# Stick-breaking attention in a hybrid trunk block: key blocks of 128 with a separate sum tile, against key blocks of 127 with the sum in row 0

## The reference, cut to what matters

```python
z = einsum('bqhd,bkhd->bhqk', q_blk, kh) * scale
mask = key_pos[None, :] < q_pos[:, None]
log_1m_beta = where(mask, log_sigmoid(-z), 0.0)
between = cumsum(log_1m_beta, axis=3, reverse=True) - log_1m_beta
weights = where(mask, exp(log_sigmoid(z) + between), 0.0)
out = einsum('bhqk,bkhd->bqhd', weights, vh)
```

## Time and profile before

| | us |
|---|---|
| median of 3 runs | 1556.61 (1551.15 to 1557.23) |
| profiled execution, time | 1550.32 |
| profiled execution, span from first to last instruction | 1548.5 |
| `heads`, first exp of a unit to the first product of `Ahead` | 522.8 to 730.6 |

### The profile page before, as it was taken

How to read it: one execution, slowest core, us unless ns; L and a number is a source line. 1 busy time by engine, 2 the same in 40 slices (tenths; PEclk the granted TensorE clock), 3 DMA queues, 4 the chain that set the end, 5 groups by cost and what they waited for, 6 DMA issues and landing times.

```text
span 1548.5 us, 27297 instructions
## 1 busy us (share of the span) xinstructions
PE 1466.1 (95%) x11281; PEld 1138.3 (74%) x11281; DVE 670.5 (43%) x1072; ACT 525.2 (34%) x947; POOL 308.9 (20%) x412
## 2 busy tenths in 40 slices
PE   7989989989898899999999999999999999999997
PEld 5767777767677555554777788888888888888876
DVE  6244151555653454655464424242332424242337
ACT  5423231433323476877443403021120403021132
POOL 6674615422332252523001000000000000000000
PEclk9999989999999999999999999999999999999999
DMA  6454413423224513021433302021120302111014
GB/s 201 138 149 120 127 42 97 125 59 86 70 68 109 166 25 78 6 76 62 163 109 109 109 0 95 14 68 41 38 70 0 98 10 75 34 57 51 27 60 171
DMA packets 134969, 124.10 MB, mean 80 GB/s; under 512 B 20829, under 2 KB 112154, under 8 KB 134874
## 3 DMA queue, kind: packets, MB, share of 16 engines
q1 hardware_dynamic: 88588, 92.90, 19.4%
q10 hardware_dynamic: 46286, 29.84, 6.8%
HBM read 97.88 MB, written 24.84 MB: 79 GB/s over the span
## 4 chain that ended last, share of the span: by engine, by line
PE 47%; DVE 2%; ACT 1%; DMA 1%; issue 1%; POOLq 0%; SPq 0%; DVEq 0%; ACTq 0%
PE all_ps_b L2018 22%; PE all_ps_b L1995 22%; PE all_ps_b L1585 2%; DMA bk_acc<-in_w_out 1%; POOLq L1605 0%; DVE bk_acc L1872 0%; PE all_ps_b L1988 0%; ACT bk_acc L1773 0%; DVE bk_acc L1882 0%; DVE bk_w1L L1843 0%; DVE bk_acc L1868 0%; DVE all_hL L1888 0%; DVE all_gL L1914 0%; ACT bk_rect L1804 0%; DVE bk_acc L1945 0%
## 5 line engine op out<-in xcount | busy, mean ns | idle before, releaser
L1924 DVE TENSOR_TENSOR bk_acc<-bk_acc,all_ps_b 128x512 f32<-128x512 f32 x128 | 87.9, 687 | 274.4 <-PE all_ps_b L2018 274.2
L1995 PE MATMUL all_ps_b<-all_hH,bk_w1L 128*128 128x512 f32 x512 | 200.2, 391 | 5.1 <-PE all_ps_b L2018 2.1
L2018 PE MATMUL all_ps_b<-bk_w2H,all_gL 128*128 128x512 f32 x512 | 199.4, 389 | 2.5 <-DVE all_gL L1914 2.5
L1995 PE MATMUL all_ps_b<-all_hH,bk_w1H 128*128 128x512 f32 x512 | 199.4, 389 | 0.0
L1995 PE MATMUL all_ps_b<-all_hL,bk_w1H 128*128 128x512 f32 x512 | 199.3, 389 | 0.0
L2018 PE MATMUL all_ps_b<-bk_w2L,all_gH 128*128 128x512 f32 x512 | 199.2, 389 | 0.0
L2018 PE MATMUL all_ps_b<-bk_w2H,all_gH 128*128 128x512 f32 x512 | 199.2, 389 | 0.0
L1207 PE MATMUL fr_ps_F<-fr_hH,fr_wL 128*128 128x512 f32 (+1 forms) x416 | 174.7, 420 | 6.5 <-POOL fr_wL L459 6.4
L459 POOL TENSOR_TENSOR fr_wL<-fr_raw,fr_wH 128x256 fp32r<-128x256 f32 (+1 forms) x208 | 161.9, 809 | 26.0 <-ACT fr_wH L504 22.7
L1207 PE MATMUL fr_ps_F<-fr_hL,fr_wH 128*128 128x512 f32 (+1 forms) x416 | 164.8, 396 | 0.0
L1207 PE MATMUL fr_ps_F<-fr_hH,fr_wH 128*128 128x512 f32 (+1 forms) x416 | 164.5, 395 | 0.0
(11 more groups left out here) (349 smaller groups left out, 2281.9 us busy)
## 6 DMA issues: line engine op xcount, KB each, us to landing
fr_raw<-in_w_in ACTq DMA_DIRECT2D x37, 512.0 KB, 4.2
bk_raw<-in_w_ff SPq DMA_DIRECT2D x32, 512.0 KB, 4.3
all_raw<-in_w_ff SPq DMA_DIRECT2D x32, 512.0 KB, 3.7
projected<-fr_stage ACTq DMA_DIRECT2D x39, 256.0 KB, 4.4
fr_raw<-in_w_in SPq DMA_DIRECT2D x13, 512.0 KB, 4.3
fr_xt<-in_x SPq DMA_DIRECT2D x8, 512.0 KB, 5.1
bk_acc<-in_x SPq DMA_DIRECT2D x8, 512.0 KB, 3.3
x_after_mixers<-bk_acc SPq DMA_DIRECT2D x8, 512.0 KB, 2.6
```

What stands on the lines that cost most here:

```text
L1924: dve.tensor_tensor(acc[:, j, ds], acc[:, j, ds], ybank[g % 4][:], ALU.add).then_inc(collected, 1)
L1995: m = pe.matmul(bank[s][h][:], w[s][:, k, :], a[:, k, hs], start=(k == 0 and q == 0), stop=(k == KB - 1 and q == 2))
L2018: m = pe.matmul(ybank[g % 4][:], a[:, i, ts], w[:, i, ds], start=(i == 0 and q == 0), stop=(i == FB - 1 and q == 2))
```

## The change

Blocks have 127 keys. Partition 0 of each tile is free, and carries the sum of the later keys of this head; one product with a mask whose row 0 is +1 (`later`) does what `tri` and `ones` did together. `R`, its adds on GpSimd, `tri`, `ones`, `unit` are gone. What replaces them is a handover: after `sums(u)` row 0 of `Z` is the sum that the next block of the head needs. VectorE copies it to a small tile `row` (`hand_on(u)`, after `softplus(u + 2)` in its queue), and GpSimd copies it into row 0 of `SP` of unit u + 2 before `sums(u + 2)`. `weight(u)` waits for the handover, counted by `handed`. Columns where the unit is the first block that a query sees have no later sum; they take a product of their own with `later_only` (row 0 is zero). The units of a pair become 10 + 18 = 28, of which 24 hand a row on; the GLA slots are counted over the 24 units that aren't first of their half, so their number is unchanged. The mask product is now F32 instead of F32R. K and V are loaded in segments of 127 columns.

```diff
     for c in range(QC):
-        for kb in range(PER * (c + 1) - 1, -1, -1):
+        top = ((c + 1) * HALF - 1) // KEYS
+        for b in range(top, -1, -1):
             for h in range(2):
-                UNITS.append((h, c, kb, max(0, (kb - PER * c) * P), kb == PER * (c + 1) - 1))
+                UNITS.append((h, c, b, max(0, (KEYS * b - c * HALF) // 2 * 2), min(P, (c + 1) * HALF - KEYS * b + 1), b == top))
...
+    def load_blocks(self, q, to, rows, src, done):
+        whole = TB * KEYS
+        q.dma_start(to[rows, 0:TB * P].rearrange("p (b c) -> p b c", c=P)[:, :, 1:P],
+                    src[:, 0:whole].rearrange("p (b c) -> p b c", c=KEYS)).then_inc(done, 16)
+        q.dma_start(to[rows, TB * P + 1:TB * P + 1 + T - whole], src[:, whole:T]).then_inc(done, 16)
...
+                e.clear(act, ident).then_inc(s("early_blank"), 1)
+                act.wait_ge(s("early_blank"), 1)
...   (GpSimd)
-                            pool.tensor_tensor(new[:, off:], old[:, off:], SP[u % 4][:, off:], ALU.add
-                                               ).then_inc(s("sum"), 1)
-                        if off:
-                            pool.memset(new[:, off - P:off], 0.0)
...
+                    if not first:
+                        known = UNITS[u - 2][3]
+                        pool.wait_ge(s("handed"), handed(i, u - 2))
+                        pool.wait_ge(s("sp"), i * NU + u + 1)
+                        pool.tensor_copy(SP[u % 4][0:1, known:HALF], row[(u - 2) % 4][0:1, known:HALF]
+                                         ).then_inc(s("placed"), 1)
+                        gla(i * NG + NTH[u] - 1)
...   (ScalarE, weight)
                     act.wait_ge(s("tri_mm"), i * NU + u + 1)
                     if u >= 4 or i:
                         act.wait_ge(s("v_mul"), i * NV + (u - 4) // 2 + 1)
+                    if hands_on(u):
+                        act.wait_ge(s("handed"), handed(i, u))
-                    act.activation(W[u % 4][:, span(u)], Z[u % NZ][:, span(u)], ACT.Exp).then_inc(s("weight"), 1)
+                    act.activation(part(W[u % 4], u), part(Z[u % NZ], u), ACT.Exp).then_inc(s("weight"), 1)
...
-                    gla(i * NU + u)
+                    if not UNITS[u][5]:
+                        gla(i * NG + NTH[u])
...   (VectorE)
+                def hand_on(i, u):
+                    if not hands_on(u):
+                        return
+                    off = UNITS[u][3]
+                    dve.wait_ge(s("tri_mm"), i * NU + u + 1)
+                    if u >= 4 and hands_on(u - 4):
+                        dve.wait_ge(s("placed"), placed(i, u - 2))
+                    dve.tensor_copy(row[u % 4][0:1, off:HALF], Z[u % NZ][0:1, off:HALF]).then_inc(s("handed"), 1)
 
                 for u in range(NU):
                     softplus(u)
+                    if u >= 2:
+                        hand_on(i, u - 2)
...
-                    gla(i * NU + u - 1)
+                    if not UNITS[u][5]:
+                        gla(i * NG + NTH[u] - 1)
...   (TensorE, scores)
-                if kb >= PER * c:
-                    m = pe.matmul(Z[u % NZ][:, off:off + P], unit[:], never[:], start=False, stop=True,
-                                  skip_group_check=True)
+                low = c * HALF + off - b * KEYS + 1
+                masked = min(P - low, HALF - off)
+                if masked > 0:
+                    m = pe.matmul(Z[u % NZ][0:rows, off:off + masked], ident[0:rows, 0:rows],
+                                  mask["never"][0:rows, low:low + masked], start=False, stop=True, skip_group_check=True)
...   (TensorE, sums)
-                    m = pe.matmul(z, tri[:], SP[u % 4][:, span(u)], start=False, stop=True, skip_group_check=True)
-                    if not first:
-                        pe.wait_ge(s("cut"), i * NU + u - 1)
-                        m = pe.matmul(z, ones[:], rd[:, span(u)], start=False, stop=True, skip_group_check=True)
+                    if off < known:
+                        m = pe.matmul(z[0:rows, off:known], mask["later_only"][0:rows, 0:rows], sp[0:rows, off:known],
+                                      start=False, stop=True, skip_group_check=True)
+                    if known < HALF:
+                        pe.wait_ge(s("placed"), placed(i, u))
+                        m = pe.matmul(z[0:rows, known:HALF], mask["later"][0:rows, 0:rows], sp[0:rows, known:HALF],
+                                      start=False, stop=True, skip_group_check=True)
```

More of the change, by code:

```diff
@@ L87, in clear @@
         self.semaphores.close()
-SB_MASKS = ("ones", "to_diag", "above", "same64")
+SB_MASKS = ("same64", "never", "later", "later_only")
+FAR = 1e30
+KEYS, KCOLS = P - 1, TB * P + 16
+USED = TB * P + 2 + T - TB * KEYS
 class Early:
@@ L408, in _ @@
             finish(LAST)
[L409 removed]
+            sp.wait_ge(s("early_v"), 32)
             left["stored"][1] = 16 * UN
@@ L2567, in sum_bank, with part, handed, hands_on @@
             return G[0] if i == LAST and n else X
-        def span(u):
-            h, c, kb, off, first = UNITS[u]
-            return slice(off, HALF)
+        def part(t, u):
+            h, c, b, off, rows, first = UNITS[u]
+            return t[0:rows, off:HALF]
+        def handed(i, u):
+            return i * NG + sum(1 for n in range(u + 1) if hands_on(n))
+        def hands_on(u):
+            return u + 2 < NU and not UNITS[u + 2][5]
+        def placed(i, u):
+            return i * NG + NTH[u + 1]
         def half(n):
@@ L2608, in _ @@
             gla = gla_pool(pool)
-            def units(i):
-                nth = [0, 0]
+            for i in range(PAIRS):
                 for u in range(NU):
[L2614 to L2625, removed]
-                            pool.tensor_tensor(new[:, off:], old[:, off:], SP[u % 4][:, off:], ALU.add
-                                               ).then_inc(s("sum"), 1)
-                        if off:
-                            pool.memset(new[:, off - P:off], 0.0)
-                    else:
-                        pool.sem_inc(s("sum"), 1)
-                    pool.drain().then_inc(s("cut"), 1)
-                    gla(i * NU + u - 1)
-            for i in range(PAIRS):
-                units(i)
+                    h, c, b, off, rows, first = UNITS[u]
+                    if not first:
[5 more added lines that the diff above has]
+                        gla(i * NG + NTH[u] - 1)
         @block.scalar
@@ L2723, in _ @@
         def _(dve):
[L2724 to L2727, removed]
             def split(i):
@@ L2835, in scores @@
                 qs = slice(c * HALF + off, (c + 1) * HALF)
[L2836 to L2842 removed]
+                z, k = Z[u % NZ][0:(rows + 1) // 2 * 2, off:HALF], kS[h][:, b * P:b * P + (rows + 1) // 2 * 2]
@@ L2866, in values @@
-                    if first and c == 1:
-                        pe.wait_ge(s("v"), i * 2 + 2)
+                    pe.wait_ge(s("v"), i * 3 + VALUES_READY[u])
                     if first and (i or c):
```

144 lines of the change are left out of this document (79 added, 65 removed).

## The result

The changed kernel takes **1612.71 us** (median of 4 runs, 1606.61 to 1615.78), the kernel before beside it 1556.92: a ratio of 1.036 (95% interval 1.033 to 1.0385), slower by 56 us. The forecast was 1592 in a range of 1548 to 1615: the sign and the range hold, the size was under-forecast, 35 for 56. The time lies just above the forecast's own range (1565 to 1612) and where rival 3 was put (1610 to 1625). The profiled execution took 1606.61 us, its span 1604.9. The first exp of a unit starts at 521.2 (before 522.8) and `heads` ends at 787.6, so the stage grew from 207.8 to 266.4 us and holds all of the loss.

What follows compares the result with a forecast made beforehand. The prediction took a ring of ScalarE and VectorE to replace TensorE as bound: 181 + 42 + 8 + 10 + 2 = 243 us against 207.8, 35 more, so 1592 us on the runs' scale; own range 1565 to 1612, for all 1548 to 1615.

Steps and rivals of the forecast that it cites:

- rival 3: In `heads`, TensorE's clock falls because it now idles: 15 to 30 us more, 1610 to 1625; chance 0.09.
- The ring: In `heads`, weight, exp, ln on ScalarE, then softplus and row copy on VectorE run in series: 181 us for three pairs.
- A plain wide turn: One 512-column turn of ScalarE and VectorE in series, including two handovers at 0.03 each: 3.09 us.
- The row copy: VectorE's one-partition copy of 512 columns: taken as 0.68 us, as partitions don't count; at 0.2, 19 us less.
- Side work: GLA pieces in `heads` where VectorE's waits for ScalarE's piece of the slot before, serial to the ring: 42 us.
- the overflow: GLA pieces that fit a wide turn but not a narrow one: about 8 us, an estimate.
- between pairs: From a pair's last handover to the next pair's first: 8.2 us instead of 3.3, 5 a boundary, 10 in all.
- TensorE's saving: `ones` products removed, 48 us, less added units, mask passes and split `sums`: net 28 us less, about 173 of 200.8.
- rival 1: TensorE stays the bound of `heads` and the net saving arrives: 1522, on the runs' scale 1529; chance 0.12.
- GpSimd: Its placing of the row, perhaps 0.6 to 0.7 us for 512 columns, costs nothing under 3.9 us of cover.
- The rival sentence on the shared port: GpSimd and VectorE operations with two SBUF inputs lock each other out; the change helps as GpSimd's adds go.
- The front: Before `heads`, loads in 508-byte segments and five small ScalarE clearings were costed at nothing; clearings up to 1 us.

Runs made afterwards that it cites:

- run 2: Changed kernel with `weight(u)` waiting only for the sums, the row copy waiting for `weight(u)`, and `scores` reusing the bank waiting for the copy: 1565.77 us, ratio 1.0057.
- run 3: Changed kernel with the row handed on one unit sooner (`u - 1` in place of `u - 2`, behind softplus): 1561.42 us, ratio 1.0036.
- run 6: Kernel before the change with one added wait, `weight(u)` also waiting for `softplus(u + 2)`, and no copy: 1584.68 us, ratio 1.0167.
- run 5: Changed kernel with copy and placing of only the row's last 4 columns, the others' later sum left out: 1589.22 us, ratio 1.0206.
- run 4: Changed kernel with VectorE's GLA pieces one slot later against ScalarE's: 1580.96 us, ratio 1.015.
- run 10: Changed kernel with the row handed on one unit sooner and only its last 4 columns copied and placed: 1546.75 us, ratio 0.9944.

## Why the prediction was right, and where it was short

**The ring** was the likeliest case and is what happened: runs 2 and 3 undo nothing but order and give back 47 and 51 of 56 us, run 6 makes a ring where there was none.

**A plain wide turn**: forecast 3.09, measured 3.17. The missing 0.08 is the handover from the row copy to `weight`. I had 0.03, from a handover out of ScalarE; the copy ends at 577.52 and `weight` starts at 577.63, 0.11. Over 72 handovers that is 6 us.

**The row copy**: taken as 0.68 between 0.2 and 0.68, measured 672 ns. That partitions don't count, read from an operation on 64 of them, holds down to one. I priced it at 0.53 more than a very short copy, 19 us; run 5 gave 23.5.

**Side work**: `keys` turns forecast at 4.3 or more, measured 4.36 three times of five, 5.47 and 5.91 in the second pair. Over the 21 wide turns that hand a row on, pieces included, the terms give 81.1 us (21 x 3.09, five `keys`, `state`, `take`, two `soft`, two `soft_g`), and the trace 82.2. That this is so close is partly luck: `soft` and `take` cost at most 0.4 of the 2.9 us put down for them, and the two long `keys` turns are 2.7 us above the others. `soft_g` and `state` cost as much as forecast.

**What was under-sized**: 266.4 - 82.2 = 184.2 us are left for the other units (called the narrow ones here, with the 512-column units of the first half) and the joints of the pairs, where the forecast has 162. The last pair, at a granted clock of 1.00, took 73.3 us, as its terms give: 60.3 for the units, 2.4 for two `both`, 3.8 for `result`, 2.7 of the overflow, 2 for the end and half a boundary, 73.7. So some 24 us are missing in the first two pairs, 4 of them handovers. About 5 are in the two joints: from the last `weight` that waits for a handover to the first of the next pair the forecast has 8.2, the trace 9.9 (604.30 to 614.21) and 11.5 (702.86 to 714.34). About 18 are in the narrow units. Run 4 shows that the order of the pieces doesn't explain them: with most pieces out of the way the first two pairs still take 80.3 and 82.9 us, where ring, overflow and boundary would make 68, and its last pair 73.5, at granted clocks of 0.89, 0.90 and 0.98. In the terms of the prediction, the 10 us "between pairs" was too small by about 5, and the narrow units with the 8 us of pieces "that fit a wide turn but not a narrow one" by about 16 beyond the handovers.

**TensorE's clock** (rival 3, 0.09) took part, which I had left out of the forecast's sum. The granted clock was 0.92 over the stage: 0.91, 0.86 and 1.00 in the three pairs, by the windows above. If what is missing from 1.00 is time at 1.2 GHz, that is about 17 and 28 us at 1.2 GHz in the first two pairs (an estimate from these rows: 0.09 x 93.0 / 0.5, and 0.14 x 100.1 / 0.5), 4 in the whole stage before, and none in the pair that came out as forecast. Four of the stretches, at the start of the second pair, in two of its `keys` turns and at the joint to the third:

```profile
624.00:640.00 16.00, 11.74 (x107) 7.57 (x107) 6.78 (x13) 7.93 (x17) 1.39 (x3) 0.79 0.59 116
675.17:680.64 5.47, 5.47 (x40) 2.40 (x34) 4.25 (x8) 2.23 (x4) 1.59 (x2) 0.62 0.00 0
687.34:693.25 5.91, 5.91 (x121) 4.62 (x118) 3.75 (x8) 2.24 (x5) 1.54 (x2) 0.52 0.01 3
704.00:718.00 14.00, 10.71 (x78) 5.56 (x78) 8.36 (x16) 7.10 (x18) 0.36 (x2) 0.78 0.37 132
```

In both `keys` turns TensorE is busy throughout. In the second its 128 GLA products (L2567) and the `sums` behind them, after the same lines of the first pair at a granted clock of 1.00:

```profile
583.12 2.07 PE L2567 MATMUL all_ps_b<-gla_D 32*64 32x32 f32 x128
586.55 1.02 PE L2901 MATMUL all_ps_b<-sb_E,all_sb_masks 128*128 128x512 f32 x2
...
686.76 3.64 PE L2567 MATMUL all_ps_b<-gla_D 32*64 32x32 f32 x128
690.33 2.08 PE L2901 MATMUL all_ps_b<-sb_E,all_sb_masks 128*128 128x512 f32 x2
```

VectorE's `take` needs these GLA products and starts at 690.52; `keys`, softplus and the row copy stand behind it. So the mechanism of the rival is real, though these two turns make only 2.7 us, and turns in which VectorE has no such piece were 3.15 to 3.18 in every pair, but for one of 3.55 in the second. How much of the 18 us in the narrow units is slow products and how much GLA pieces in the way of the ring was not separated, and stays open: the pair that had no low clock also has few GLA pieces. The Trainium skill (TensorE: Matmul & The Clock Gate, Part 1) ties the low rate to an idle TensorE. The trace agrees in part: in the 5 us before the fall at 686 it was busy for 2.9 us, its longest pause 1.9; but from 760 to 787 it was busy for 17.8 of 27 us and stayed at 1.00.

**TensorE's saving**: forecast 28, and 25 by the records of `sums` and mask together (129.2 to 104.5), 20 over the stage with `scores` and `values` (228.0 to 207.8), which grew by 12 more units and ran at a lower clock. As busy time nothing was saved in the stage, 203.3 us for 200.8, where the forecast had 173; run 10, with the same products at a granted clock of 0.98, has 184.4, so that at nearly full clock the saving is about 16. The split was the dear part: 120 records of 0.295 us for the 128 columns or fewer in which no row is taken over. None of it reached the time of the changed kernel, and rival 1 (1529) fell.

**GpSimd** was rightly costed at nothing: the placing takes 0.60 us, in the mean 819 ns, within 3.9 us of cover; TensorE waited for it for 2.6 us in all. The rival sentence on the shared port went the right way: with GpSimd's adds gone the `keys` products take 0.425 us, where they had 0.549 in the mean and 1.23 at worst.

**The front**: longer segments and clearings cost nothing that can be told; the stage began 1.6 us sooner, but in run 4, with the same front, at 525.1.

## What to carry to other kernels

Before giving an engine's bulk work to a small operation elsewhere, write down who waits for that operation and what stands ahead of it in its queue: here one wait on a copy of one partition closed a ring of five operations on two engines and cost 56 us, twice what the removed products were forecast to be worth. When a stage slows while its old bound idles, undo the order first and the work last; one index (`u - 1` for `u - 2`) gave back 51 of 56 us. And a cure belongs to its bound: later slots won 32 us in the ring and lost 17 outside it.

## What the runs showed of the hardware

- A VectorE copy from PSUM of 1 partition and 512 columns takes 672 ns, one of 128 partitions 0.68 us; 262 columns take 411 ns, 4 columns 146 ns.
- A handover from VectorE to ScalarE took 0.11 us, one from ScalarE to VectorE 0.03.
- GpSimd's copy of a 1x512 row takes 0.60 us, and 1.54 where VectorE's subtraction of two SBUF tiles (L1605) begins in it. In run 3 this alternates, and VectorE's operation (730.15 to 730.82) keeps its 0.67:

```profile
729.75 1.54 POOL L2660 COPY sb_E<-sb_row 1x512 f32<-1x512 f32 x1 [2.42 <-DVE sb_E L2797]
731.55 0.60 POOL L2660 COPY sb_E<-sb_row 1x512 f32<-1x512 f32 x1 [0.26 <-DVE sb_E L2797]
```

  By the Trainium skill (SBUF — State Buffer, "SBUF: two separate sides") such operations exclude each other, and the one that starts first keeps the shared port pair. The trace agrees that they get in each other's way, but not on who waits: GpSimd's copy began 0.40 us sooner and is the one held up. In the ring this was hidden; with the row handed on sooner it lies in the chain.
- TensorE's 128 products of 32 columns (L2567) took 2.07 us at a granted clock of 1.00 and 3.64 in a stretch at 0.52; the two passes of a 512-column F32 product 1.02 and 2.08.
